# Half of the expert hidden products moved beside selection and gate spreading, and gate products written to every fourth PSUM column

## The reference, cut to what matters

```
q = (x @ w_q).reshape(N, 8, 2, 128)
s = einsum("nhcd,ckd->nhck", q, sub_keys)
s1, i1 = top_k(s[:, :, 0], 16);  s2, i2 = top_k(s[:, :, 1], 16)
cand_s = s1[..., :, None] + s2[..., None, :]     # 256 sums per head
top_s, pos = top_k(cand_s, 16)
idx = (i1 * 128 + i2) at pos                     # expert number
gate = softmax(top_s)
act = gelu(einsum("thkd,td->thk", u_tab[idx], x)) * gate
out = einsum("thk,thkd->td", act, v_tab[idx])
```

## Time and profile before

| | us |
|---|---|
| median of 3 runs | 3643.89 (3641.54 to 3648.51) |
| profiled execution, first to last instruction | 3646.5 |
| TensorE busy in it | 3253.8 (89%) |
| VectorE busy | 1872.8 (51%) |
| ScalarE busy | 1183.3 (32%) |

### The profile page before, as it was taken

How to read it: one execution, slowest core, us unless ns; L and a number is a source line. 1 busy time by engine, 2 the same in 40 slices (tenths; PEclk the granted TensorE clock), 3 DMA queues, 4 the chain that set the end, 5 groups by cost and what they waited for, 6 DMA issues and landing times. The chain is left out here.

```text
span 3646.5 us, 46239 instructions
## 1 busy us (share of the span) xinstructions
PE 3253.8 (89%) x17304; PEld 2795.8 (77%) x17304; DVE 1872.8 (51%) x3994; ACT 1183.3 (32%) x1817; POOL 15.6 (0%) x24
## 2 busy tenths in 40 slices
PE   8995693998999999999996888556999999999997
PEld 2795392456999999999995857545999999999996
DVE  0324669664444444444445445998444444444445
ACT  0332010675322222223332331069323333333331
POOL 0000000000000000000000000000000000000000
PEclk9996896999999999999997899789999999999998
DMA  7321020765444444443431202034544444444450
GB/s 288 128 75 70 18 95 0 277 217 223 141 153 144 164 137 152 148 164 135 150 110 70 99 12 94 1 139 184 196 141 164 150 146 141 164 146 150 141 174 19
DMA packets 135421, 485.05 MB, mean 133 GB/s; under 512 B 5856, under 2 KB 105376, under 8 KB 108448
## 3 DMA queue, kind: packets, MB, share of 16 engines
q1 hardware_dynamic: 133920, 480.55, 36.9%
q10 hardware_dynamic: 1152, 3.20, 0.2%
q0 software_dynamic: 256, 0.07, 0.0%
HBM read 430.18 MB, written 53.61 MB: 133 GB/s over the span
## 5 line engine op out<-in xcount | busy, mean ns | idle before, releaser
L1088 PE MATMUL hidden_ps<-h_hi,u_hi 128*128 128x384 f32 x2048 | 688.7, 336 | 17.9 <-DVE u_lo L1151 17.9
L1088 PE MATMUL hidden_ps<-h_hi,u_lo 128*128 128x384 f32 x2048 | 688.9, 336 | 0.0
L1088 PE MATMUL hidden_ps<-h_lo,u_hi 128*128 128x384 f32 x2048 | 687.4, 336 | 0.0
L1104 PE MATMUL out_ps<-v_hi,act_lo 128*128 128x512 f32 x1536 | 602.7, 392 | 0.0
L1104 PE MATMUL out_ps<-v_lo,act_hi 128*128 128x512 f32 x1536 | 602.1, 392 | 0.0
L1104 PE MATMUL out_ps<-v_hi,act_hi 128*128 128x512 f32 x1536 | 597.2, 389 | 0.0
L1156 DVE TENSOR_TENSOR v_lo<-v_slot,v_hi 128x1024 fp32r<-128x1024 f32 x256 | 313.8, 1226 | 500.9 <-ACT v_hi L1124 500.9
L1124 ACT ACTIVATE v_hi<-v_slot 128x1024 fp32r<-128x1024 f32 x256 | 271.1, 1059 | 675.9 <-PE out_ps L1104 675.9
L1166 DVE TENSOR_TENSOR act<-gelu,w_ring 128x384 f32<-128x384 f32 x256 | 143.0, 558 | 620.1 <-ACT gelu L1130 620.1
L1088 PEld LDWEIGHTS hidden_ps<-h_hi,u_hi 128*128 128x128 f32 x2048 | 385.9, 188 | 27.9 <-ACT u_hi L1118 18.1
L1088 PEld LDWEIGHTS hidden_ps<-h_lo,u_hi 128*128 128x128 f32 x2048 | 385.7, 188 | 9.8
(11 more groups left out here) (300 smaller groups left out, 3374.9 us busy)
## 6 DMA issues: line engine op xcount, KB each, us to landing
u_slot<-in_peer_u SPq DMA_DIRECT2D x64, 2048.0 KB, 8.2
v_slot<-in_peer_v SPq DMA_DIRECT2D x64, 2048.0 KB, 8.4
ada_w_ring<-in_ada_w SPq DMA_DIRECT2D x24, 2048.0 KB, 8.8
spread_gates<-spread SPq DMA_DIRECT2D x24, 2048.0 KB, 6.3
w_ring<-spread_gates SPq DMA_DIRECT2D x64, 768.0 KB, 7.0
even_w_ring<-in_even_w SPq DMA_DIRECT2D x16, 1024.0 KB, 4.9
peer_wq<-in_peer_w_q SPq DMA_DIRECT2D x8, 2048.0 KB, 17.5
odd_w_ring<-in_odd_w SPq DMA_DIRECT2D x6, 1536.0 KB, 6.5
```

The lines of the kernel that those rows point to most:

```text
L1088: mm = pe.matmul(PH_[:, b, 0:T], u[:, b, k * P:(k + 1) * P], x[:, k, :], start=(k == 0 and n == 0), stop=(k == KB - 1 and n == 2))
L1104: mm = pe.matmul(PO[:, t, c, :], a[:, b, t * P:(t + 1) * P], x[:, b, c * CH:(c + 1) * CH], start=(first and jj == 0 and n == 0), stop=(las ...
```

## The change

`peer_select` and `peer_gates` become one block, `peer_front`, and `peer_experts` is rebuilt around it. The memory of a PEER layer is laid out by hand (`Map`), so that tiles of the stages share addresses.

- **u-products early.** The u-products of blocks 0 to 63 (EARLY = 64) are computed in `peer_front`: 16 beside the selection (SEL_N), then 9, 3, 3 and 4 between the steps of the key numbers and gates (TAIL_N), one behind each of the 24 groups of 16 tokens of the gate stage (GATE_N), and 5 at the end (LAST_N). Their gelus go to DRAM (`HD`, 16 stores of 768 KB) and are read back in `peer_experts`, which takes blocks 64 to 127 first, as before, and then blocks 0 to 63 with no u-product.
- **Queries** are computed in the fast format in three parts, for all 384 tokens at once: 16 groups of 24 products of 384 columns, where weights are split on ScalarE and VectorE first.
- **Selection** takes one key half for three token tiles at a time; pair sums go head by head. Digits and softmax are done once for all tokens. The comparisons that build one-hots and digits read their scalar operand as pairs of equal bf16 numbers.
- **Gates.** For 16 tokens at a time VectorE makes a bf16 one-hot of the second key (RM), one of the first (L), and three products of RM with the high, middle and low part of the gate (R): five instructions of 2048 elements. TensorE adds up three bf16 products for a token, and writes them to every fourth column of the PSUM bank (`k:CH:4`), so that the copy by ScalarE reads it in order.
- **Modulation rows** of layer 1 (layer 0 only) are computed beside the selection, in pieces of four products of 256 columns that go to four places of PSUM's partitions (0, 32, 64, 96).

The core of the diff. First TensorE's part of the front, and ScalarE's copy:

```diff
+                    def gates(h):
+                        pe.wait_ge(lr_ready, h + 1)
+                        for q in range(4 * h, 4 * h + 4):
+                            if q >= 4:
+                                pe.wait_ge(w_taken, q - 3)
+                            for k in range(4):
+                                tok = 4 * (q % 4) + k
+                                for part in range(3):
+                                    mm = pe.matmul(PW[:, q % 4, k:CH:4], L[:, h % 2, tok, :], R[:, h % 2, part, tok, :],
+                                                   start=(part == 0), stop=(part == 2))
+                            mm.then_inc(w_done, 1)
...
+                    for b in range(SEL_N):
+                        query(b)
+                        if ada is not None:
+                            mod_piece(3 * b)
+                        if b:
+                            scores(b - 1)
...
+                        hidden(b)
...
+                    n = SEL_N
+                    for t, few in enumerate(TAIL_N):
+                        for _ in range(few):
+                            hidden(n)
+                            n += 1
...
+                    for h in range(GATE_N):
+                        gates(h)
+                        hidden(n)
+                        n += 1
+                    for _ in range(LAST_N):
+                        hidden(n)
+                        n += 1
...
+                        act.activation(WS[:, g % 2, :, 4 * k:4 * k + 4], PW[:, q % 4, :].rearrange("p (j t) -> p j t", t=4),
+                                       ACT.Copy).then_inc(w_taken, 1)
```

Then VectorE's part, in the order in which it is written out:

```diff
+                    def low_part(n):
+                        dve.wait_ge(uh, n + 1)
+                        dve.tensor_tensor(UL[:, n % 2, :], U[n // JC % 2][:, n % JC, :], UH[:, n % 2, :].bitcast(F32),
+                                          ALU.subtract).then_inc(ul, 1)
...
+                    def one_hots(h):
+                        if h >= 2:
+                            dve.wait_ge(w_done, 4 * (h - 2) + 4)
...
+                        v.mark(dve.tensor_tensor(pairs(RM[:, :, :]), each(I2), keys, ALU.is_equal))
+                        dve.tensor_tensor(pairs(L[:, h % 2]), each(I1), keys, ALU.is_equal)
+                        v.wait()
+                        for part, g in enumerate((G1, G2, G3)):
+                            ins = dve.tensor_tensor(pairs(R[:, h % 2, part]), pairs(RM[:, :, :]), each(g), ALU.mult)
+                        ins.then_inc(lr_ready, 1)
+                        dve.wait_ge(lr_ready, h + 1)
...
+                    query_low(0)
+                    query_low(1)
+                    low_part(0)
...
+                    for b in range(SEL_N):
+                        low_part(b + 1)
+                        if b + 2 < SEL_N:
+                            query_low(b + 2)
+                        if b:
+                            select_keys(b - 1)
+                            if b % 2 == 0:
+                                select_pairs(b // 2 - 1)
+                    n = SEL_N + 1
+                    low_part(n)
+                    select_keys(SEL_N - 1)
+                    low_part(n + 1)
+                    select_pairs(PH - 1)
+                    low_part(n + 2)
+                    softmax_in()
+                    digits()
+                    low_part(n + 3)
...
+                    digit_pairs()
+                    low_part(n + 4)
...
+                    n += 5
+                    for t in range(TT):
                         for c in range(2):
+                            key_numbers(t, c)
+                            low_part(n)
+                            n += 1
+                            key_sums(t, c)
+                            if c == 0:
+                                low_part(n)
+                                n += 1
+                    low_part(n)
+                    for t in range(TT):
+                        split_gate(t)
+                    low_part(n + 1)
+                    n += 2
+                    one_hots(0)
+                    for h in range(GATE_N):
+                        if n < EARLY + 2:
+                            low_part(n)
+                            n += 1
+                        if h + 1 < GATE_N:
+                            one_hots(h + 1)
+                    while n < EARLY + 2:
+                        low_part(n)
+                        n += 1
```

The u-product on TensorE (`hidden_products`) waits for the high and the low part of its block (`uh` and `ul` of at least n + 1) and then runs the same 24 products as before. In `peer_experts` the block order and the step without a u-product are new:

```diff
+                ORDER = [*range(EARLY // JC, CHUNKS), *range(EARLY // JC)]
...
+                    hidden(EARLY)
+                    for o in range(N_KEYS):
+                        if o + 1 < N_KEYS and BLOCKS[o + 1] >= EARLY:
+                            hidden(BLOCKS[o + 1])
+                        outs(o)
```

More of the change, by code:

```diff
@@ L208, in load_ahead, with transpose_modulate @@
                 sp.dma_start(to, source).then_inc(landed, 16)
-        def transpose_modulate(HT, l, first, split=None, ahead=()):
+        def transpose_modulate(HT, l, first, split=None, ahead=(), COLS=None):
             with ExitStack() as st:
@@ new lines, in build, with hidden_products @@
+        TAIL_N, GATE_N, LAST_N = (9, 3, 3, 4), T // 16, 5
+        assert SEL_N + sum(TAIL_N) + GATE_N + LAST_N == EARLY
+        def hidden_products(pe, PH_, UH, UL, HH, HL, n, uh, ul, g_done, h_done):
+            pe.wait_ge(uh, n + 1)
+            pe.wait_ge(ul, n + 1)
+            if n >= 2:
+                pe.wait_ge(g_done, n - 1)
+            b = n % 2
+            for k in range(KB):
+                for part, (u, x) in enumerate(((UH, HH), (UH, HL), (UL, HH))):
+                    mm = pe.matmul(PH_[:, b, 0:T], u[:, b, k * P:(k + 1) * P], x[:, k, :],
+                                   start=(k == 0 and part == 0), stop=(k == KB - 1 and part == 2))
+            mm.then_inc(h_done, 1)
@@ new lines, in _ @@
+                    high_part(0)
+                    high_part(1)
+                    for b in range(SEL_N):
+                        query_rows(b)
+                        if b + 2 < SEL_N:
+                            query_high(b + 2)
+                        if b:
+                            score_rows(b - 1)
+                        gelu(b)
+                        if ada is not None:
+                            for half in range(halves_by(b - 1) if b else 0, halves_by(b)):
+                                mod_row(half)
@@ new lines, in _ @@
+                    score_rows(SEL_N - 1)
+                    n = SEL_N
+                    for t, few in enumerate(TAIL_N):
+                        for i in range(few):
+                            gelu(n)
+                            n += 1
+                            if t == 0 and i == 4:
+                                act.wait_ge(e_in, 1)
+                                act.activation(TV[:, :, :, :], TV[:, :, :, :], ACT.Exp).then_inc(e_out, 1)
+                        if t < TT:
+                            pick_rows(t)
@@ L1092, in step, with hidden @@
[L1092 to L1100 removed]
+                    def hidden(n):
+                        hidden_products(pe, PH_, UH, UL, HH, HL, n, uh, ul, g_done, h_done)
```

840 lines of the change are left out of this document (436 added, 404 removed).

## The result

The changed kernel takes 3838.73 us (median of 4 runs, 3836.65 to 3844.84) beside 3644.7 us for the kernel before: ratio 1.0538 [1.0521, 1.0555], 194 us slower. The prediction was 3890 us, range 3730 to 4110. The profiled execution has a span of 3837.7 us and a mean granted clock of 0.916.

A forecast was written before the change was run, and what follows sets the result against it. TensorE was taken to bound 58% of the span (expert stages), with neither engine full in the fronts. Layer 0 +114.3 and layer 1 +133.4 us gave +247.7 on a span of 3646.5, hence 3890 us, range 3730 to 4110.

The forecast's parts named there:

- Expert stages: Both layers: 64 full steps of 8.31 us and 64 output-only steps of 4.2 us, 800.6 us a stage.
- Selection: Fronts: 16 turns, in layer 1 9.3 us each, bound by TensorE (149 us), in layer 0 13.1 us each (209.6 us).
- the modulation: Layer 0's selection: 12 products a turn, 5.8 us one after another or 1.5 side by side; 3.3 taken.
- Tail: From the end of u-product 15 to the end of gates(0), at VectorE's pace: 100 us.
- The turn: Gate stage: one-hots, low part, u-product and gate products follow one another, 19.6 us a turn, 21 turns 411.6 us.
- The gate products: Gate stage: 48 products a group start 0.12 us apart, set by the weight load, 5.8 us.
- my lower bound of 0.067: Gate stage: time of a 128-column product in us, from its columns and a fixed part; 3.2 us a group.
- the second rival: Gate stage: the stride slows gate products to 0.229 us each, 250 us more, 4140 us; chance 0.13.
- Pairs: VectorE's five one-hot instructions of 2048 elements, reading pairs, take 1.22 us each.
- End behind gates(21): Layer 1's front: one more idle time, two gate groups and eight u-products, 54.5 us.
- the two rivals at 4140: Gate products slowed by the stride (chance 0.13), or pairs not speeding VectorE, 2.29 us instead of 1.22 (chance 0.07).
- The first rival: Gate stage: low parts keep ahead of the one-hots wait, turn 10.0 us, kernel 3480 us; chance 0.08.

The follow-up runs named there:

- e7_mod_one_place: Changed kernel with the four modulation products of a piece sent to the same partitions and added up there: 3898.41 us, ratio 1.0697.
- e5_filler: Changed kernel with 36 useless products into an unused PSUM bank behind each group of gate products: 3779.02 us, ratio 1.0369.
- e2_dense_psum: Changed kernel with gate products written to dense PSUM columns and ScalarE's copy turning four tokens: 3749.34 us, ratio 1.0289.
- e4_low_ahead_single: e1_low_ahead with the lists of the gates' left-hand side read element by element, not in pairs: 3579.49 us, ratio 0.9821.
- e1_low_ahead: Changed kernel with one more low part of u made in the gate loop's second pass, each later one a turn earlier: 3430.64 us, ratio 0.9414.
- e10_no_u_in_gates: Changed kernel with 24 u-products a layer taken out of the gate stage and left in the expert stage: 3456.95 us, ratio 0.9485.
- e11_dense_no_u_in_gates: Changed kernel with dense gate product columns and 24 u-products a layer left in the expert stage, none between gates: 3448.98 us, ratio 0.9463.

## Why the prediction was right, step by step

The direction and the mechanism were right, and the forecast 51 us too high. By its own terms:

- **Expert stages.** Predicted 800.6 us each, measured 798.9 and 798.7. The output-only step is 4.14 and not 4.2: the helpers keep up, and TensorE sets it. For layer 0 I took 1063.5 us from a window that ends 1.9 us before the last product (1939.86 in the kernel before), so the saving is 266.5 in both layers and not 263.
- **Selection.** Layer 1: 9.02 us a turn (predicted 9.3) behind a first one of 10.15, 145.6 us from the first query instead of 151. Layer 0: 11.94 a turn, alternately 11.73 and 12.15 (predicted 13.1), behind a first one of 17.32; 195.7 instead of 211.6. The greater part of layer 0's difference is the modulation, where I took the middle of 1.5 and 5.8 us a turn; e7_mod_one_place shows that the low end holds (three pieces at 0.61). The Trainium skill ("TensorE: Matmul & The Clock Gate", section "Why this matters for your kernels") says that narrow outputs at partitions 32 apart land in column groups of their own and run at once; the two rows of 0.61 and 1.89 us agree, a factor of 3.1 for four.
- **Tail.** 103.0 and 101.1 us; predicted 100. That many small estimates came so near is in part luck, since their errors cancel: in layer 1 VectorE waited 3.0 us for high parts of u between them, which the sum doesn't have, and the gate splits took 5.7 us and not 6.2.
- **The turn**, predicted 19.6, measured 18.83. TensorE's idle time 7.16 (7.6: five one-hots start 1.135 us apart where I took 1.2, which is most of it), the u-product with the clock 6.25 on average (4.2 + 2.0; shown by e5_filler's 2.0), gate products 5.42 (5.8). 21 turns are 395 us and not 412: 16 of the 20 to 29 us by which I had a front too long.
- **The gate products** were nearly right in size and wrong in the reason. I took 0.12 us from the earlier trace rows because I held the weight load for the limit. I also misread that row: it counts records, and a plain float product makes two (1536 records for 768 gate products in the kernel before), so its eight were four products. Dense, bf16 products with weights of the same shape are 0.056 apart, even below my lower bound of 0.067, and the gaps make it 0.109. That two errors gave nearly the right number was luck. So the second rival was true as a mechanism and wrong in its price: a gapped column costs as much as two, not as four. The Trainium skill's rule ("PSUM — Partial Sum Buffer", specifications) that gaps in the output slow matmuls is borne out by e2_dense_psum, with a factor of 1.9.
- **Pairs.** 1.22 us as predicted; e4_low_ahead_single shows that the single form would have cost 2.29.
- **The rest.** End behind gates(21) 53.6 and 52.7 us (54.5), then 8.3 and 7.5 us until the expert stage (5). In layer 0 the splitting of the first query weights lay beside the end of the stage before, so its 2.5 us cost 0.3.
- **The range.** By my own list 0.34 lay outside 3730 to 4110 (0.08, 0.06, and 0.20 for the two rivals at 4140), where I wrote about 2 in 10. The range was narrower than my chances allowed.

Sum: layer 0's front is 756.2 us against 407.9, layer 1's 704.7 against 326.6; 348.3 + 378.1 - 2 x 266.5 = 193.4, and 2.3 us less between the layers give the 191.2 by which the spans differ (predicted 247.7).

The mechanism is shown from two sides: one low part ahead of the wait (e1_low_ahead), or no u-product between the gates (e10_no_u_in_gates), and the turn is no longer serial. The first rival (the low parts don't get stuck) stands on the other side of the sign, by one instruction: it was priced at a turn of 10.0 us and 9.6 us saved in each; e1_low_ahead has 9.42 and saves 9.41.

## What to carry to other kernels

Where two engines feed each other through double buffers, write down for one turn which item each engine has finished when it comes to a wait: a single item on the wrong side of a wait makes the turn the sum of both engines' work, and the profile shows it as two engines that are both partly idle in one stretch. Don't count on both waits naming the other engine: here the profile named the gate product for VectorE's wait, but gave "issue" for TensorE's. Fill an idle engine with moved work only after the turn has been looked at: here the same u-product cost 13.0, 3.6 or 1.3 us of a turn by where its low part stood and how the gate products were written. And weigh a layout that makes one engine's copy cheap (595 instead of 1088 ns on ScalarE, which was hidden either way) against what it costs the engine that is the bound.

## What the runs showed of the hardware

- A bf16 product of 128 columns with its own weights starts every 0.056 us into dense PSUM columns and every 0.109 us into every second or every fourth column.
- A u-product takes 4.17 us where TensorE has no idle time. Behind an idle time of 7.2 us in each turn it takes alternately 5.7 and 6.7 us, at a granted clock of 0.80; with 36 useless products in the idle time 4.25. Where TensorE worked less in a turn (e2_dense_psum) it takes 7.0, at 0.71.
- Shorter idle times can cost the same: in e4_low_ahead_single TensorE idles 2.0 us of a turn of 12.27, the granted clock of 780 to 1037 us is 0.94, and of the u-products behind 2.6 us of idleness some take 5.7 to 5.8 us and others 4.24. There it cost nothing, since VectorE set the turn.
- In e11_dense_no_u_in_gates TensorE was busy 119 of 184 us of the gate stage (743.9 to 928) at a granted clock of 0.88, without any effect on the turn, which is 5.80 us as in e10_no_u_in_gates: VectorE set it.
- Four products to partitions 0, 32, 64 and 96 took 0.61 us, the same four to one place 1.89.
